# Hybrid encoder step: token blocks of the mixers reordered, layer norm per block

## What is computed

```
h = rms_norm(x, norm_g);  u = h @ w_in                              # 1536 columns
a = u[:, :512] * sigmoid(u[:, 512:1024])
y = depthwise_conv(concat(history, a), conv_w)                      # 31 taps, 512 channels
c = silu(layer_norm(y + conv_b) * ln_g + ln_b)
z = ((windowed_mean(u[:, 1024:]) - u[:, 1024:]) @ pool_w[g]) * pool_scale   # 4 groups
x = x + concat(c, z) @ w_out                                        # 1024 x 1024
h = rms_norm(x, norm_ffn)
layer 0:  x = x + (silu(h @ w_gate) * (h @ w_up)) @ w_down          # dense, width 2816
layer 1:  logits = h @ router_w + router_b; top 2 of 8 experts, each a SwiGLU of width 2816
return rms_norm(x, norm_final), new histories
```

## Time and profile before

| | before |
|---|---|
| median of three runs | 1390.68 us |
| profiled execution | 1390.41 us, its span 1388.5 us |
| TensorE busy | 1322.4 us (95%) |
| VectorE busy | 1015.4 us (73%) |
| ScalarE busy | 804.4 us (58%) |
| GpSimd busy | 107.3 us (8%) |
| DMA | 373.68 MB, 269 GB/s |

### The profile page before, as it was taken

How to read it: one execution, slowest core, us unless ns; L and a number is a source line. 1 busy time by engine, 2 the same in 40 slices (tenths; PEclk the granted TensorE clock), 3 DMA queues, 4 the chain that set the end, 5 groups by cost and what they waited for, 6 DMA issues and landing times.

```text
span 1388.5 us, 15532 instructions
## 1 busy us (share of the span) xinstructions
PE 1322.4 (95%) x6107; PEld 1100.5 (79%) x6108; DVE 1015.4 (73%) x1061; ACT 804.4 (58%) x805; POOL 107.3 (8%) x157
## 2 busy tenths in 40 slices
PE   5998899999998998779999999999999999999995
PEld 4996788888886997658888888888888888888884
DVE  4887633333334778668888988888888888888895
ACT  4554422222323472447777777777777777777772
POOL 1060300000000050220000000000000000000120
PEclk9999999999999999979999999999999999999998
DMA  9215498333233304349999999999999999999991
GB/s 322 76 32 190 151 404 308 123 127 132 72 102 104 120 16 156 125 168 399 388 374 394 376 374 378 390 373 375 387 374 380 384 373 382 377 372 371 386 381 48
DMA packets 179199, 373.68 MB, mean 269 GB/s; under 512 B 7084, under 2 KB 59748, under 8 KB 179126
## 3 DMA queue, kind: packets, MB, share of 16 engines
q1 hardware_dynamic: 167878, 335.78, 66.7%
q0 software_dynamic: 9456, 34.75, 6.6%
q10 hardware_dynamic: 1792, 2.18, 0.4%
HBM read 345.85 MB, written 26.82 MB: 268 GB/s over the span
## 4 chain that ended last, share of the span: by engine, by line
PE 85%; DVE 10%; ACT 2%; issue 1%; DMA 1%; POOL 0%; SPq 0%; DVEq 0%; POOLq 0%
PE ps L324 27%; PE ps L326 27%; PE ps L325 27%; DVE ps L921 5%; PE ps L1335 1%; DMA raw<-in_w_in 1%; DVE w_lo L304 1%; DVE ext L881 1%; ACT ext L562 1%; PE ps L1521 1%; DVE x L1015 1%; DVE a_lo L888 1%; PE ps L1417 1%; PE ps L1292 1%; POOL stat L1602 0%
## 5 line engine op out<-in xcount | busy, mean ns | idle before, releaser
L304 DVE TENSOR_TENSOR w_lo<-raw,w_hi 128x2048 fp32r<-128x2048 f32 x317 | 724.7, 2290 | 144.5 <-ACT w_hi L619 87.9
L619 ACT ACTIVATE w_hi<-raw 128x2048 fp32r<-128x2048 f32 x264 | 506.3, 1919 | 145.0 <-PE ps L326 145.0
L324 PE MATMUL ps<-w_hi,xT_hi 128*128 128x512 f32 x704 | 279.6, 397 | 1.4 <-DVE xT_lo L980 1.4
L326 PE MATMUL ps<-w_hi,xT_lo 128*128 128x512 f32 x704 | 275.3, 391 | 0.0
L325 PE MATMUL ps<-w_lo,xT_hi 128*128 128x512 f32 x704 | 274.4, 390 | 0.0
L326 PEld LDWEIGHTS ps<-w_hi,xT_lo 128*128 128x128 f32 x704 | 132.1, 188 | 28.5
L324 PEld LDWEIGHTS ps<-w_hi,xT_hi 128*128 128x128 f32 x704 | 132.3, 188 | 27.6 <-DVE xT_lo L980 1.6
L325 PEld LDWEIGHTS ps<-w_lo,xT_hi 128*128 128x128 f32 x704 | 132.4, 188 | 26.5
L324 PE MATMUL ps<-w_hi,a_hi 128*128 128x512 f32 x360 | 142.1, 395 | 3.4 <-DVE ft_lo L941 2.1
L326 PE MATMUL ps<-w_hi,a_lo 128*128 128x512 f32 x360 | 140.3, 390 | 0.0
L325 PE MATMUL ps<-w_lo,a_hi 128*128 128x512 f32 x360 | 140.1, 389 | 0.0
(11 more groups left out here) (193 smaller groups left out, 1497.5 us busy)
## 6 DMA issues: line engine op xcount, KB each, us to landing
raw<-in_moe_w_down SPq DMA_DIRECT2D x88, 1024.0 KB, 7.4
raw<-in_moe_w_gate SPq DMA_DIRECT2D x80, 1024.0 KB, 7.3
raw<-in_moe_w_up SPq DMA_DIRECT2D x80, 1024.0 KB, 7.2
raw<-in_w_in SPq DMA_DIRECT2D x12, 1024.0 KB, 11.9
x_rows<-ext POOLq DMA_DIRECT2D x6, 2048.0 KB, 24.8
...
```

Source lines behind the costliest of these rows:

```text
L304: dve.tensor_tensor(slot(w_lo, s), slot(raw, s), slot(w_hi, s).bitcast(F32), ALU.subtract)\
L324: pe.matmul(out, lh, rh, start=start, stop=False)
L326: return pe.matmul(out, ll, rh, start=False, stop=stop)
L619: act.activation(slot(w_hi, s), slot(raw, s), ACT.Copy).then_inc(hi_ready[s], 1)
```

## The change

The three token blocks go in the order samples, prompt 0, prompt 1 (`TB_ORDER`) in every norm, turn, w_out and dense unit. The convolution is divided anew: VectorE takes the samples of tiles 0 and 1 and the prompt of tile 0 (part a), then the prompt of tiles 1 and 2 (part c); TensorE takes the samples of tiles 2 and 3 and the prompt of tile 3. The layer norm is made per block with tokens on partitions: TensorE turns y (`turn_y`), VectorE takes mean and variance (`moments`) and GpSimd the power (`ln_scale`), ScalarE normalizes, TensorE turns back (`turn_back`), ScalarE applies gain, bias and silu. The sums over partitions, the square root and the reciprocal are gone. w_out runs block by block. The first tiles of what follows (w_in of layer 1, the dense stage, the experts) are split earlier. The logits come with tokens on partitions, in one accumulation for each block, and need no turn. Slots and PSUM banks are assigned anew.

The core of the diff:

```diff
+TB_ORDER = [2, 0, 1]
+OUT_BANK = [2, 4, 0]
...
-        def wanted(c, shift):
-            return c + shift < NF
+        def wanted(kind, c, shift, end=NF):
+            return c + shift < (end if kind == "d" else end + 1)
...
+            rows = [xp[0], xp[1], a["x_sample"].rearrange("s t d -> (s t) d")]
+            for tb in TB_ORDER:
+                sp.dma_start(x[:, tb * D:(tb + 1) * D], rows[tb]).then_inc(S[f"x_loaded{tb}"], 16)
...
+                def bias(c):
+                    return prm[:, C_CB + 4 * l + c:C_CB + 4 * l + c + 1]
+                def normalize(i):
+                    tb = TB_ORDER[i]
+                    act.wait_ge(S["shift_ready"], NTB * l + i + 1)
+                    act.activation(y_all(i), ln_psum(i), ACT.Identity, scale=ln_rstd[:, tb:tb + 1],
+                                   bias=ln_shift[:, tb:tb + 1]).then_inc(S["yn_ready"], 1)
+                def gain_silu(i):
+                    act.wait_ge(S["yn_turned"], NTB * l + i + 1)
+                    for c in range(NCB):
+                        ins = act.activation(y_sb(i, c), ps[:, LN_BANK[i], c * P:(c + 1) * P], ACT.Silu,
+                                             scale=prm[:, C_LG + 4 * l + c:C_LG + 4 * l + c + 1],
+                                             bias=prm[:, C_LB + 4 * l + c:C_LB + 4 * l + c + 1])
+                    ins.then_inc(S["c_done"], 1)
+                    act.wait_ge(S["c_done"], NTB * l + i + 1)
+                    act.activation(ht_view(a_hi, TB_ORDER[i], 0), y_all(i), ACT.Copy).then_inc(S["c_hi"], 1)
+                act.wait_ge(S["conv_a_done"], l + 1)
+                act.wait_ge(S["pe_conv_done"], 3 * l + 2)
+                act.wait_ge(S["st_turned"], NST * (l + 1))
+                for c in range(NCB):
+                    ins = act.activation(y_sb(0, c), ps[:, 3, c * P:(c + 1) * P], ACT.Identity, bias=bias(c))
+                ins.then_inc(S["y_ready"], 1)
+                make_hi(act, WOUT_SLOT[2], GEN_WOUT[l][2])
+                normalize(0)
...
+                gain_silu(0)
...
+                make_hi(act, WOUT_SLOT[3], GEN_WOUT[l][3])
+                act.wait_ge(S["c_lo"], NTB * l + 1)
+                act.activation(ext[:, LN_ROWS:LN_ROWS + SEQ], ps[:, 4, 0:SEQ], ACT.Identity, bias=bias(0))
+                act.wait_ge(S["pe_conv_done"], 3 * l + 3)
+                act.activation(ext[:, LN_ROWS + 3 * SEQ:LN_ROWS + 4 * SEQ], ps[:, 5, 0:SEQ], ACT.Identity, bias=bias(3))
...
-                for c in range(NCB):
-                    act.wait_ge(S["xn_done"], 4 * l + c + 1)
-                    act.activation(y_sb(c), y_sb(c), ACT.Silu, scale=prm[:, C_LG + 4 * l + c:C_LG + 4 * l + c + 1],
-                                   bias=prm[:, C_LB + 4 * l + c:C_LB + 4 * l + c + 1]).then_inc(S["c_done"], 1)
-                for c in range(NCB):
-                    act.wait_ge(S["c_done"], 4 * l + c + 1)
-                    act.activation(a_hi[:, c * TOK:(c + 1) * TOK], y_sb(c), ACT.Copy).then_inc(S["c_hi"], 1)
...
+                act.wait_ge(S["conv_c_done"], l + 1)
+                for c in (1, 2):
+                    o = LN_ROWS + c * SEQ
+                    ins = act.activation(ext[:, o:o + SEQ], ps[:, 2, (c - 1) * SEQ:c * SEQ], ACT.Identity, bias=bias(c))
+                ins.then_inc(S["y_ready"], 1)
+                normalize(1)
+                normalize(2)
+                if l:
...
+            def moments(l, i):
+                tb = TB_ORDER[i]
+                dve.wait_ge(S["y_turned"], NTB * l + i + 1)
+                link(dve.bn_stats(out=bn[:, 6 * tb:6 * tb + 6], in_=ps[:, LN_BANK[i], :]))
+                link(dve.bn_aggr(out=mean_var[:, 2 * tb:2 * tb + 2], in_=bn[:, 6 * tb:6 * tb + 6]))
+                dve.tensor_scalar(ln_ve[:, tb:tb + 1], mean_var[:, 2 * tb + 1:2 * tb + 2], EPS, None, ALU.add)\
+                   .then_inc(S["ve_ready"], 1)
+            def shift(l, i):
+                tb = TB_ORDER[i]
+                dve.wait_ge(S["ln_rstd_ready"], NTB * l + i + 1)
+                dve.tensor_scalar(ln_shift[:, tb:tb + 1], mean_var[:, 2 * tb:2 * tb + 1], ln_rstd[:, tb:tb + 1], -1.0,
+                                  ALU.mult, ALU.mult).then_inc(S["shift_ready"], 1)
+            def c_low(l, i):
+                tb = TB_ORDER[i]
+                dve.wait_ge(S["c_hi"], NTB * l + i + 1)
+                dve.tensor_tensor(ht_view(a_lo, tb, 0), y_all(i), ht_view(a_hi, tb, 0).bitcast(F32), ALU.subtract)\
...
                 gated(l, 1)
-                conv(l, [(0, False), (0, True)], 0, 6)
+                part_a = [(0, True), (1, True), (0, False)]
+                dve.wait_ge(S["gated"], 4 * l + 2)
+                dve.wait_ge(S["hist_ready"], 2 * NCB * (l + 1))
+                conv(l, part_a, 0, 12)
                 make_lo(dve, WOUT_SLOT[0], GEN_WOUT[l][0])
-                conv(l, [(0, False), (0, True)], 6, TAPS)
+                conv(l, part_a, 12, TAPS)
+                dve.wait_ge(S["conv_step"], steps[0])
+                dve.sem_inc(S["conv_a_done"], 1)
+                part_c = [(1, False), (2, False)]
                 gated(l, 2)
-                conv(l, [(1, False), (1, True)], 0, 7)
+                make_lo(dve, WOUT_SLOT[1], GEN_WOUT[l][1])
+                dve.wait_ge(S["gated"], 4 * l + 3)
+                dve.wait_ge(S["st_copied"], NST * l + 2)
+                conv(l, part_c, 0, 3)
                 gated(l, 3)
-                conv(l, [(1, False), (1, True)], 7, TAPS)
-                conv(l, [(2, True), (3, True)], 0, TAPS)
+                conv(l, part_c, 3, 15)
+                moments(l, 0)
+                conv(l, part_c, 15, 19)
+                shift(l, 0)
+                conv(l, part_c, 19, 22)
+                make_lo(dve, WOUT_SLOT[2], GEN_WOUT[l][2])
+                conv(l, part_c, 22, 25)
+                c_low(l, 0)
                 for g in range(NCB):
                     dve.wait_ge(S["z_hi"], 4 * l + g + 1)
                     o = (4 + g) * TOK
                                              scalar=prm[:, C_PS + 4 * l + g:C_PS + 4 * l + g + 1],
                                              in1=a_hi[:, o:o + TOK].bitcast(F32), op0=ALU.mult,
                                              op1=ALU.subtract).then_inc(S["z_lo"], 1)
-                dve.wait_ge(S["mean_done"], l + 1)
-                for c in range(NCB):
-                    dve.tensor_tensor(y_sb(c), y_sb(c), ps[:, 6, 0:TOK], ALU.subtract).then_inc(S["xc_done"], 1)
-                for s in range(1, 4):
...
-                dve.wait_ge(S["sd_ready"], l + 1)
...
                 n = 2 * l + 1
+                early_lo(0)
+                moments(l, 1)
+                moments(l, 2)
+                shift(l, 1)
+                shift(l, 2)
                 add(0)
                 mean_square(n, 0)
...
+                c_low(l, 1)
                 norm_row(n, 0)
-                if l == 0:
...
-                    expert_lo(MAIN[0], 1)
+                c_low(l, 2)
+                if l:
+                    dve.wait_ge(S["rw_hi_ready"], 1)
+                    dve.tensor_tensor(rw_lo[:, :], rw_raw[:, :], rw_hi[:, :].bitcast(F32), ALU.subtract)\
+                       .then_inc(S["rw_lo_ready"], 1)
+                early_lo(1)
+                dve_hT(n, 0)
...
+                def conv_samples(i):
+                    c = 2 + i
                     pe.wait_ge(S["gated"], 4 * l + c + 1)
+                    for j in range(TAPS):
+                        pe.wait_ge(S["diag_ready"], (2 * l + i) * TAPS + j + 1)
+                        ins = pe.matmul(streams(ps[:, 3, c * P:(c + 1) * P]), diag[i][:, j * P:(j + 1) * P],
+                                        c_sample(c, j, DSEQ), start=j == 0, stop=j == TAPS - 1)
+                    ins.then_inc(S["pe_conv_done"], 1)
...
+                def conv_prompt(first, end):
                     for j in range(first, end):
...
+                pe.wait_ge(S["hist_ready"], 2 * NCB * (l + 1))
+                pe.wait_ge(S["conv_a_done"], l + 1)
+                conv_samples(0)
                 pe.wait_ge(S["gated"], 4 * (l + 1))
-                for n in range(NPST, NST):
-                    states(n)
-                conv(1, 0, 20)
+                for i in range(NPST, NST):
+                    states(i)
+                conv_samples(1)
+                conv_prompt(0, 8)
+                turn_y(0)
+                conv_prompt(8, 22)
+                turn_back(0)
...
+                conv_prompt(22, TAPS)
                 pe.wait_ge(S["z_lo"], 4 * (l + 1))
-                pe.wait_ge(lo_ready[WOUT_SLOT[0]], GEN_WOUT[l][0] + 1)
-                for tb in range(NTB):
-                    ins = w_out(0, tb)
-                ins.then_inc(S["wout_used"], 1)
-                pe.wait_ge(S["sq_done"], 4 * (l + 1))
-                for c in range(NCB):
-                    ins = pe.matmul(ps[:, 7, 0:TOK], mean_w[:, :], y_sq(c), start=c == 0, stop=c == NCB - 1)
-                ins.then_inc(S["var_done"], 1)
```

(45 more changed lines are left out.)

383 lines of the change are left out of this document (186 added, 197 removed).

## The result

The changed kernel takes 1381.99 us (median of four runs, 1381.32 to 1383.22), the kernel before 1390.42 in the same comparison: ratio 0.994, interval 0.9925 to 0.9955. It is 8.4 us faster. Forecast was 1369, range 1361 to 1381: the sign is right, the size is not, and the time lies just above the range. The profiled execution took 1383.22 us with a span of 1381.4.

The account below looks back on a forecast made before the run. TensorE was taken as bound, with an unchanged 759 us expert stage and waits for normalized rows ahead of it. Gains 7.2 + 1.3 + 6.3 + 6.8 = 21.6 took 1390.4 to 1368.8, with 0.3 to the median 1369; range 1361 to 1381.

Parts of the forecast that it names:

- Both mixers: Convolution start to w_out's end 71.8 us for 78.1; gains 7.2 us in the first mixer, 6.3 in the second.
- Rival C: Mixers: weight loads set the sample taps' price, slower from 0.20 us a pass; 1394 us, chance 0.06.
- rival D: Mixers: VectorE's stand and ScalarE's queue eat the layer norm's gain, only crossings stay; 1386 or above, chance 0.06.
- Rival B: Mixers: TensorE is the only bound, w_out can start earlier; 1361 us, chance 0.11.
- Head of the second mixer: Crossing from dense loop to second mixer: earlier w_in splits remove one w_lo from VectorE, gain 1.3 us.
- Router: After w_out's end: logits there 11 us later instead of 17.9, gain 6.8 us.
- Now two thirds of the logits are done early: Router: only the last block's norm, turn, splits and 24 products were counted after w_out's end.
- rival A: Mixers and router: half clock after TensorE's waits and semaphore latency cost 8 us; 1377 us, chance 0.22.
- The price of a product, 0.06 to 0.12: Router: step in us of the last block's 24 products of 8 columns, 1.4 to 2.9 us in all.
- Start: Ahead of the first mixer: sample rows load first, history later; gain taken as 0, bounds -0.6 and +1.8 us.
- From the dense units on nothing changes: Dense units after the first mixer: nothing changes but which slot a tile has.
- 759 us: Expert stage: its length was to stay unchanged at 759 us.

Follow-up runs that it names:

- stand: Changed kernel with nine more pairs of VectorE convolution taps ahead of the sample block's statistics; one execution of 1381.47 us.
- z_first: Changed kernel with ScalarE's pooled-channel copies and VectorE's low parts of them moved ahead of those of the sample block's silu; 1379.26 us.
- z_split: On top of z_first, TensorE makes five prompt taps between the second and third pool product; 1377.67 us.
- r_hyb: Changed kernel with per-block logits, but router_w's 8 columns stationary and the block's 128 moving, each block copied and turned; 1375.0 us.
- best: Changed kernel with r_hyb, z_split and eps joined, all logits turned behind the last block, and expert tile 2 split earlier; 1369.35 us, ratio to before 0.9854.
- hist_early: Changed kernel with the history loads issued after the first power instead of after all three, as before; one execution of 1384.0 us.
- eps: Changed kernel with an unused 4-byte tensor where the removed eps was, restoring the addresses behind it; 1380.63 us.
- pad: Changed kernel with 64 one-column memsets on VectorE at the start; one execution of 1380.6 us.

## Why the prediction was right or wrong

**Both mixers: right.** Counted from the first tap, w_out's end was put at 71.8 us; it came at 72.0 in both layers. The chain through TensorE's passes, VectorE's stand and ScalarE's queue is the one in the rows, and `stand` and `z_first` show which of its links bind: ScalarE's order does, VectorE's stand doesn't. Rival C (0.2 us a pass) and rival D are out. Rival B, TensorE alone as the bound, isn't the changed kernel either, but `z_split` comes near it and gets only a third of what it should, for the next link is late by then. The first mixer gave 6.4 for 7.2: the first dense unit came 73.6 us after the first tap, half a microsecond later than counted, and from there to the third unit's first product it took 14.4 us as before, for which the count had 14.2. The addends for w_out's end make 149.6, not 149.8. GpSimd's powers were rightly counted as nothing: all 21 take 0.55 to 0.57 us, and the two of 2.54 in the kernel before have gone.

**Head of the second mixer: right,** 1.2 for 1.3.

**Router: wrong, and this is the step that failed.** Forecast was 11.1 us after w_out's end, measured 19.1. Step by step, from w_out's end at 569.75 in the changed kernel:

| step | counted | measured |
|---|---|---|
| until the last block's normalized rows are ready | 5.7 | 6.1 |
| until TensorE turns them | 0 | 4.0 |
| turn and splits, to the block's first product | 2.4 | 3.4 |
| its 24 products | up to 2.9 | 5.1 |
| from there to the maximum | 0 | 0.5 |

Two terms of the sum failed. "Now two thirds of the logits are done early" gave the second block's logits no price, but they stand ahead of the last block's turn in TensorE's queue, and the rows waited 4.0 us for them. And turn and products were priced at the full clock, with 2.3 us for its fall in rival A alone, while it was at half from 574.7 to 598.6. The kernel before had half clock at this place too, from 588.3 to 598.5; its turn of the last block took 1.97 us where the prediction took 0.9:

```profile
590.24 1.97 PE L1261 MATMUL ps<-ident,ext 128*128 128x128 f32 x8 [4.42 <-DVE ext L881]
```

The shares of the two can be estimated. With the 2.7 us of the first block, at full clock, the second block's logits would have ended at 577.4, 1.5 us behind the rows instead of 4.0. So of the 8.0 us missing, some 5.7 are the half clock (2.5, 1.0 and 2.2), 1.5 the order, and the rest small terms. What made the clock fall at 574.7 isn't isolated. It came after the first block's 24 products and 0.5 us of idle time, and in all seven kernels with the router of the change it fell between 571.2 and 575.7. In `r_hyb`, with shorter products and longer waits between them, it stayed full to 583.2, but in `best`, with the same products, only to 574.8.

The price of a product, 0.06 to 0.12, was not the failed step: it holds the 0.112 of the full clock, and the 11.1 us come out with its upper end. But the argument for its lower end was a misreading. The three turns that start 0.06 apart load 128 columns of 8 rows; the products load 128 columns of 128 rows, and the transposes of that shape, 0.11 in the same trace, were the nearer row. The stretch at half clock, and the start of the experts, in the changed kernel (columns as above):

```profile
574.70:598.60 23.90, 17.14 (x77) 16.58 (x78) 12.04 (x50) 8.56 (x9) 0.58 (x1) 0.50 0.20 67
604.50:608.70 4.20, 4.15 (x12) 3.25 (x13) 2.29 (x1) 0.63 (x1) 3.59 (x3) 0.61 0.98 366
```

`r_hyb`, with the operands exchanged, has 13.1.

**Start: unpriced gain.** Bounds of -0.6 to +1.8, taken as 0, measured +2.6, outside them; `hist_early` gives 2.3 us of it back at the first product and 1.7 at the first tap, so the later history loads are most of it.

**What was taken as unchanged wasn't.** "From the dense units on nothing changes" and "759 us" fail by 1.4 and 2.9 us. The dense loop's 1.4 and most of 1.3 in the expert stage are the address of the tensors behind `eps` (see that run). The other 1.6 of the expert stage's 2.9 are the clock, 0.61 of full until 608.7 in this execution: its first expert chunk takes 16.0 us, that of all other kernels here 14.4. In w_in of the second layer the clock was at half for the first 6.1 us of the products, for 4.1 before, which is 1.0 us. The rows are of the changed kernel, then of the kernel before:

```profile
442.30:448.40 6.10, 6.10 (x19) 6.10 (x20) 4.49 (x2) 2.81 (x2) 0.00 (x0) 0.50 0.01 3
```

```profile
451.10:455.20 4.10, 4.08 (x13) 4.08 (x14) 4.10 (x2) 3.43 (x2) 0.00 (x0) 0.50 0.84 272
```

The tail's 2.3 us go away with 64 more instructions (`pad`), most likely by where VectorE's code lies. Rival A had 8 us for the cold array: 4.6 in the middle of the mixers, where the clock stayed full, 2.3 in the router, where it fell, and 1.1 for semaphore latency, for which no row stands. So its 1377 was nearer than the forecast partly by luck. What remains open: why 32 bytes matter, why the clock fell at 574.7, and whose instructions are loaded while VectorE stalls.
